# Where a feed-forward kernel's weights and activations start modulo 256 bytes

## The reference

```python
x = x + 0.5 * swiglu(rms_norm(x, norm_ffn1[l]), ffn1_w_gate[l], ffn1_w_up[l], ffn1_w_down[l])
x = x + hybrid_mixer(rms_norm(x, norm_mix[l]), ...)
x = x + 0.5 * swiglu(rms_norm(x, norm_ffn2[l]), ffn2_w_gate[l], ffn2_w_up[l], ffn2_w_down[l])

def swiglu(x, w_gate, w_up, w_down):
    return (jax.nn.silu(x @ w_gate) * (x @ w_up)) @ w_down
```

## The kernel before

| piece | stationary | moving |
|---|---|---|
| A11 B11, A12 B21 | gate panel, `w_hi`/`w_lo` | `xg_hi`/`xg_lo` |
| S2 T2, S3 T3, S1 T1 | sums of weights, `ws_hi`/`ws_lo` | sums of x quarters, `xs_hi`/`xs_lo` |
| A22 T4 | second half of the up panel, `w_hi`/`w_lo` | `xs_hi`/`xs_lo` |
| S4 B22 | sums of weights, `ws_hi`/`ws_lo` | `xg_hi`/`xg_lo` |

## Time and profile before

### The profile page before, as it was taken

How to read it: one execution, slowest core, us unless ns; L and a number is a source line. 1 busy time by engine, 2 the same in 40 slices (tenths; PEclk the granted TensorE clock), 3 DMA queues, 4 the chain that set the end, 5 groups by cost and what they waited for, 6 DMA issues and landing times. The chain is left out here.

```text
span 2542.8 us, 38480 instructions
## 1 busy us (share of the span) xinstructions
PE 2443.6 (96%) x15217; PEld 2122.1 (83%) x15217; DVE 1703.4 (67%) x2316; ACT 1129.8 (44%) x1586; POOL 422.3 (17%) x450
## 2 busy tenths in 40 slices
PE   7997997999999999999999999999999999999998
PEld 6876776789897878878898979999888887899996
DVE  5355996668786444467786878787843446687776
ACT  5343884434343223545353554344422346544443
POOL 0002111622111500011121102121051001121110
PEclk9997998999999999999999999999999999999999
DMA  4125996246554321135565546565332213465652
GB/s 145 59 67 181 381 413 236 75 137 155 149 135 127 108 83 53 50 106 150 145 167 148 124 126 175 137 171 143 115 115 84 75 42 91 128 163 145 163 141 78
DMA packets 120713, 348.69 MB, mean 137 GB/s; under 512 B 16066, under 2 KB 21074, under 8 KB 120274
## 3 DMA queue, kind: packets, MB, share of 16 engines
q1 hardware_dynamic: 81634, 245.48, 29.1%
q0 software_dynamic: 38032, 98.06, 16.5%
q10 hardware_dynamic: 864, 2.62, 0.3%
HBM read 331.95 MB, written 12.58 MB: 135 GB/s over the span
## 5 line engine op out<-in xcount | busy, mean ns | idle before, releaser
L522 DVE TENSOR_TENSOR w_lo<-w_raw,w_hi 128x1024 fp32r<-128x1024 f32 (+2 forms) x353 | 421.8, 1195 | 143.3 <-ACT w_hi L517 142.0
L517 ACT ACTIVATE w_hi<-w_raw 128x1024 fp32r<-128x1024 f32 (+2 forms) x353 | 352.7, 1004 | 357.0 <-PE bank_l L566 331.3
L566 PE MATMUL bank_l<-xg_hi,w_hi 128*128 128x512 f32 x872 | 346.1, 397 | 4.9 <-DVE xg_lo L629 4.8
L566 PE MATMUL bank_l<-xg_hi,w_lo 128*128 128x512 f32 x872 | 339.9, 390 | 0.0
L566 PE MATMUL bank_l<-xg_lo,w_hi 128*128 128x512 f32 x872 | 339.8, 390 | 0.0
L566 PE MATMUL bank_l<-hid_hi_ff,w_hi 128*128 128x512 f32 x704 | 275.6, 392 | 4.8 <-DVE hid_lo_ff L654 4.6
L566 PE MATMUL bank_l<-hid_lo_ff,w_hi 128*128 128x512 f32 x704 | 274.4, 390 | 0.0
L566 PE MATMUL bank_l<-hid_hi_ff,w_lo 128*128 128x512 f32 x704 | 274.2, 389 | 0.0
L2019 ACT ACTIVATE ws_hi<-ws_raw 128x1024 fp32r<-128x1024 f32 x142 | 150.6, 1061 | 274.1 <-DVE ws_raw L2141 151.1
L1879 PE MATMUL bank_s<-xs_hi,ws_hi 128*128 128x256 f32 x852 | 238.0, 279 | 3.4 <-DVE ws_lo L2108 3.0
L1879 PE MATMUL bank_s<-xs_lo,ws_hi 128*128 128x256 f32 x852 | 236.0, 277 | 0.0
(11 more groups left out here) (454 smaller groups left out, 5702.5 us busy)
## 6 DMA issues: line engine op xcount, KB each, us to landing
ws_raw<-in_ff_up POOLq DMA_DIRECT2D x213, 256.0 KB, 4.2
w_raw<-in_ff_gate SPq DMA_DIRECT2D x88, 512.0 KB, 4.2
expert_raw<-in_experts SPq DMA_DIRECT2D x81, 512.0 KB, 18.2
w_raw<-in_in SPq DMA_DIRECT2D x80, 512.0 KB, 3.5
w_raw<-in_ff_down SPq DMA_DIRECT2D x64, 512.0 KB, 4.4
ws_raw<-in_ff_gate POOLq DMA_DIRECT2D x71, 256.0 KB, 5.5
up_raw<-in_ff_up SPq DMA_DIRECT2D x71, 256.0 KB, 2.9
w_raw<-in_out SPq DMA_DIRECT2D x24, 512.0 KB, 3.6
```

The source lines that it names most:

```text
L517: act.activation(split_memory(i)[0], split_part(i), ACT.Copy).then_inc(*panel_hi.done(i))
L522: dve.tensor_tensor(lo, split_part(i), hi.bitcast(F32), ALU.subtract).then_inc(*panel_lo.done(i))
L566: done = pe.matmul(dst, w[:, c * cols:(c + 1) * cols], moving, start=c == 0 and n == 0, stop=c == kc - 1 and n == 2)
```

## The change

Modulo 256 the starts of the operands of block products move like this (worked out from the sizes in the order of allocation):

| tensor | before | after |
|---|---|---|
| `xg_hi`, `xg_lo` (the norm of x, split) | 128 | 128 |
| `xs_hi`, `xs_lo` (sums of quarters) | 64 | 128 |
| `ws_hi`, `ws_lo` (sums of weights) | 128 | 192 |
| gate panel and up half of a block, in `w_hi`, `w_lo` | 128 | 192 |
| every other panel in `w_hi`, `w_lo` | 128 | 128 |
| `w_raw`, `up_raw`, `ws_raw`, `x_scratch`, `hid_hi_ff`, `hid_lo_ff` | 128 | 128 |

A ring place of `w_hi` and `w_lo` grows from 4096 to 4352 bytes, so that a panel can start 64 bytes into it. To make room, `strict`, `suffix` and `minus` (used in the first block only) go into a part of memory that is free then. On every engine the instructions, their order, their waits and their shapes are the same 19960 as before; only addresses differ.

```diff
+SHIFT = 16
...
-        w_hi = sb(stack, "w_hi", [P, SPLIT, PANEL], F32R)
-        w_lo = sb(stack, "w_lo", [P, SPLIT, PANEL], F32R)
+        w_hi = sb(stack, "w_hi", [P, SPLIT, PANEL + 64], F32R)
+        w_lo = sb(stack, "w_lo", [P, SPLIT, PANEL + 64], F32R)
...
-        strict = sb(stack, "strict", [P, P])
-        suffix = sb(stack, "suffix", [P, P])
-        minus = sb(stack, "minus", [P, P])
...
             route_parts = sb(phase, "route_parts", [P, 2, PANEL], F32R)
+            strict = sb(phase, "strict", [P, P])
+            suffix = sb(phase, "suffix", [P, P])
+            minus = sb(phase, "minus", [P, P])
...
-            sb(phase, "before_xs", [P, 48])
             xs_hi = sb(phase, "xs_hi", [P, 4, DC // 2, T // 2], F32R)
             xs_lo = sb(phase, "xs_lo", [P, 4, DC // 2, T // 2], F32R)
-            sb(phase, "behind_xs", [P, 16])
...
+            sb(phase, "before_ws", [P, SHIFT])
             ws_hi = sb(phase, "ws_hi", [P, 4, PANEL // 2], F32R)
             ws_lo = sb(phase, "ws_lo", [P, 4, PANEL // 2], F32R)
...
             if slot_of_panel[i][0] == "up":
-                return w_hi[:, ring_of[i], PANEL // 2:], w_lo[:, ring_of[i], PANEL // 2:]
+                at = slice(PANEL // 2 + SHIFT, PANEL + SHIFT)
+                return w_hi[:, ring_of[i], at], w_lo[:, ring_of[i], at]
+            if by_seven(i):
+                at = slice(SHIFT, PANEL + SHIFT)
+                return w_hi[:, ring_of[i], at], w_lo[:, ring_of[i], at]
             return w_hi[:, ring_of[i], 0:kc * cols], w_lo[:, ring_of[i], 0:kc * cols]
```

## The result

The changed kernel takes 2546.09 us (median of 20 runs, 2542.59 to 2552.73) against 2541.57 us (20 runs, 2537.74 to 2546.43) for the kernel before: ratio 1.0021, 95% interval [1.0015, 1.0028]. It is 4.5 us slower, where 2538.0 was forecast, and lies above the range of 2533.5 to 2542.

The account below looks back on a forecast made before the run. DVE's 10.15 us cycle, not PE's 9.76 us block, was taken to bound runs of blocks once PE's lead melts; 0.7 + 3.0 + 0 = 3.7 us off the median 2541.67 gave 2538.0, range 2533.5 to 2542.

Parts of the forecast that it names:

- Block products: PE's 84 matmuls of a block all at 113.3 ns: 0.24 us less a block, 17.0 us of PE time over 71.
- rivals 3 and 4: Moving operand's chunk distance sets the speed, no change, 2541.7, 10%; or its own start does, 2559.6, 7%.
- bounds of the unknown: Limits set for the block products' effect: no saving, and a loss of 0.32 us a block.
- rival 4: Moving operand's own start decides, 64 fast, 128 slow: 0.32 us more a block, about 18 us, 2559.6; chance 7%.
- a pattern of 512 bytes: First mixer's equal chunk times (2.92 us) taken to show addresses repeat after 256 bytes, so wider ring places cost nothing.
- What of it reaches the end: DVE's 10.15 us cycle limits gains: runs of 8 0.18 each, of 6 0.75, of 5 0; sum 3.7 us.
- Rival 1: Run's end not tied to DVE, only PE's lead counts: 6.4 us gained, 2535.3; chance 12%.
- rival 2: DVE's cycle is no bound, all 17.0 us of PE's saving arrives: 2524.7; chance 6%.
- some 11 us of PE's time turn into waits for 2108: Of PE's 17.0 us saved, 13.3 become waits, some 11 for line 2108.
- ACT and DVE at the new addresses: ACT and DVE accessing `w` and `ws` at 192 beside raw data at 128: nothing, at most 3 us either way.
- `strict`, `suffix`, `minus`: Moved constants: same transfers and reads, no new wait, so nothing.
- Ring places of 4352 bytes: Other panels keep their start modulo 256 but not 512: nothing for down products and mixers.
- The rule against the change: The skill's independent PE read ports would mean no change (2541.7); not followed, because the timeline shows two speeds.

Follow-up runs that it names:

- e1: Changed kernel with the gate panel alone back at 128 modulo 256; 2550.11 us, ratio 1.0036 to the kernel before.
- e3: Changed kernel with every operand of a block at 128, difference 0 in all pieces; 2557.97 us, ratio 1.0063 to the kernel before.
- e5: Changed kernel with `xg` moved from 128 to 192, the pattern of before shifted by 64 bytes; 2545.52 us, ratio 1.0014 to the kernel before.
- e15: Kernel before mirrored: `xs` at 192 with S1, S2, S3 and up half at 0; 2541.07 us, ratio 1.0001.
- e6: Kernel before with `xg` moved to 64, so all block pieces have difference 64; 2559.64 us, ratio 1.0075.
- e4: Changed kernel with all starts modulo 256 as before; wider ring places and moved constants kept; 2541.88 us, ratio 1.0003 to the kernel before.
- e8: Changed kernel with block panels and `ws` at 64 instead of 192, difference minus 64; 2543.97 us, ratio 1.0015 to the kernel before.
- e14: Block products all at difference 64: `xs` 64 against weights 128, `xg` 128 against 192; 2539.48 us, ratio 0.9997 to the kernel before.
- e16: Block products all at difference 64: `xs` 0 against weights 64, `xg` 128 against 192; 2542.81 us, ratio 1.0005 to the kernel before.
- e2: Changed kernel with the gate panel of only each run's first block back at 128; 2545.44 us, ratio 1.0018 to the kernel before.
- e13: As e14, but the gate panel of each run's first block at 128; 2538.49 us, ratio 0.9992 to the kernel before.
- e17: Kernel before without the last two matmuls of A12 B21 in each block, addresses unchanged; 2537.4 us, ratio 0.9982.
- e18: Kernel before without the last four matmuls of A12 B21 in each block; 2537.36 us, ratio 0.9985.

## Why the prediction was wrong

**Block products: wrong, and this is the step that failed.** "I take the difference as the cause, so that all 84 matmuls of a block run at 113.3 ns." Half of it held: difference 0 gave 120 ns in the gate pieces of every kernel that had it there, wherever the pair lay (before, e1, e3, e5, e15), and the move to 64 took that away. But difference 64 has a second rhythm of 117.8 ns, and nearly all of the changed kernel runs in it. The term "A11 B11 and A12 B21 save 0.08 each, S2 T2 0.02, S4 B22 0.06" measured 0.03, 0.03, -0.03 and 0.01, and the three pieces priced at nothing lose 0.05 each: unrounded, 0.13 us more a block in place of 0.24 less. With the difference, rivals 3 and 4 were too simple as well: e3 speaks against the one, e5 against the other. The bounds of the unknown, "no saving, and a loss of 0.32", did contain it, but I gave the loss to rival 4 alone, at 7%.

What could have told me stood in the trace of before. In the timeline of PE, behind the wait for the sums in a run of 5, piece A22 T4, at the addresses at which it otherwise takes 1.36:

```profile
1229.09 0.28 PE L1879 MATMUL bank_s<-xs_hi,w_hi 128*128 128x256 f32 x1
...
1230.50 0.28 PE L1879 MATMUL bank_t<-xg_hi,ws_hi 128*128 128x256 f32 x1
```

1.41 us. Ten `xs` pieces of before are like this, each behind a wait; the other 274 settle at 113.3. I had read one undisturbed block and taken its speeds for properties of addresses.

The first mixer, though its shapes are mixed, spoke against it too. Its moving chunks are 2112 bytes apart, so chunks 0 to 3 stand at differences 0, -64, 128 and 64, and the earlier trace rows has the ends of that stretch, 40.09 and 43.01. In between begin chunk 1 and chunk 3:

```profile
40.82 0.28 PE L566 MATMUL bank_l<-in_hi,w_hi 128*128 128x256 f32 x1
...
42.28 0.28 PE L566 MATMUL bank_l<-in_hi,w_hi 128*128 128x256 f32 x1
```

Chunk 0 and chunk 3 take 0.73 us each for six matmuls of 264 columns in the mean: difference 64 is no faster there than 0. I had used this stretch only to rule out a pattern of 512 bytes.

**Which rhythm comes: shown in part.** Shown: it is not the absolute starts (e5 and e6 against the changed kernel and before), not the ring (e4), not the speed just before alone (e1). Behind 512-column down products the pieces began at 117.8 wherever difference 64 or -64 came first (changed kernel, e6, e8, e14, e16). A step of the moving operand inside the block, up or down, behind pieces at 120 led to 113.3 (before, e5, and e15, where the weights step by 128 with it). A step of the weights alone led to 117.8 (e1, e2). Where both operands step by 64 together, down led from 117.8 to 113.3, and up led to 117.8 behind either rhythm (e13, e14). The changed kernel gives `xg` and `xs` one start, so it removes the step that had brought the fast rhythm. Why a step does this, and why e16's first blocks are an exception, stays open; so does what a wait leads to, since both rhythms were found behind waits.

**What of it reaches the end: right, but worked out for the wrong sign.** DVE's cycle stayed at 10.15 us. With a block of 9.52 (e17) the gains of the runs were 0.23 and 0.86 where this account, with the saving in A12 B21, gave 0.24 and 0.81, and 4.3 us in all for 4.2. That the sum agrees so closely is luck: e17's interval is 2.5 to 6.9, and e18 gave 4.3 for 6.1. Rival 1 (7) lies just above that interval, and the run of 8 without late transfers, in which it expected 0.5, speaks against it; rival 2 (17) is out. The forecast that some 11 us of PE's time turn into waits for 2108 was too high: they are 8.4 us in e17 against 3.0 before. For a slower PE the account says the reverse, and I had used it so only in rival 4: no DVE step waits long for PE, but PE's lead of 0.26 to 1.05 grows, and its loss arrives nearly whole. The pair of profiled executions has it run by run. The four runs of 6 lose 3.2 together. The four runs of 8 have 1.07 more in their blocks each, of which 0.3 comes back from a wait for the last hidden value; two of them had lost 1.35 and 0.65 to late transfers before, which fall away, so that the four lose 1.0 together. The runs of 5, which wait anyway, come to 0.9. Together this is 5.1 us (5.2 as counted above), for 4.5 in the medians; what late transfers do differs from one execution to the next. e3, at +0.32 a block, cost 16 where this sum gave 18.

**ACT and DVE at the new addresses, `strict`, `suffix`, `minus`: right.** DVE's rest of a pair takes 1225 ns on average after as in the earlier trace rows:

```profile
L2112 DVE TENSOR_TENSOR ws_lo<-ws_raw,ws_hi 128x1024 fp32r<-128x1024 f32 x142 | 173.9, 1225 | 48.3 <-ACT ws_hi L2023 41.3
```

**Ring places of 4352 bytes: right** by e4, which also carries the moved constants.

**The rule against the change.** e6 differs from before by starts alone and is 18 us slower; e3 has the wider ring places and the moved constants besides, which cost nothing in e4, and is 16 us slower. The Trainium skill (SBUF — State Buffer, section Who interferes with whom) gives the moving operand and the weight loads ports of their own and says that PE waits on nobody. By that rule the three kernels would take the same time; the measurement decides, and they do not.

## What to carry to other kernels

Two operands of a 256-column product with the same start modulo 256 cost 120 ns a matmul here against 113.3 or 117.8 at a difference of 64, but the way out has more than one state: look at the distances behind waits and behind other products before a speed is put down to an address. Look for the moves that a layout makes, not only for where it stands; making two starts equal took away a step that did good. And where PE lives on a lead over DVE, work the account out for both signs: 0.24 us less a block brought 4 us of 17, 0.13 more cost half of its 9. Of all layouts tried, e13's is the fastest at 2538.49 us, ratio 0.9992 [0.9983, 1.0001], no sure gain over the kernel before.

## What the hardware showed unexpectedly

- 256-column products of float32r at one difference of 64 bytes run either at 113.3 or at 117.8 ns. The changed kernel keeps 117.8 through whole runs of 8 blocks and 113.3 for more than a block, from one wait to the next. Difference 0 gives 120.0, difference 128 120.0 or 118.7.
- Products of 512 columns want the opposite: 226.8 ns at difference 0, 228.9 at -64, 233.3 at +64 in the same stretch of 336 (without its first distance). A layout that is good for the blocks costs 4.6 or 14 us there if it moves `xg` alone.
